# A mixture-of-experts decoder layer: in wide jobs VectorE turns the next job's rows in 32x32 blocks

## The chip, the cores and the metric

One NeuronCore of a Trainium2 chip runs the whole layer. The metric is the device time of one execution, in microseconds, as the median of three runs: 2102.54 us before the change (2101.25 to 2103.78).

## What is computed

The layer projects 1024 tokens of width 1024, runs sliding-window attention and a gated recurrence, projects back, and then routes each token to 4 of 32 experts. This case is about the experts only:

```python
logits = h @ router_w + router_b
top_v, top_e = lax.top_k(logits, 4)
gates = softmax(top_v)
# for every expert e, over the tokens routed to it:
hid = xblk @ w1[e] + b1[e]                      # 1024 -> 2048
glu = minimum(hid[:, 0::2], 7.0)
lin = clip(hid[:, 1::2], -7.0, 7.0)
act = glu * sigmoid(1.702 * glu) * (lin + 1.0)
y[tokens of e] += gate * (act @ w2[e] + b2[e])  # 1024 -> 1024
return rmsnorm(x + y, final_g)
```

All inputs are float32, and so is the output.

## The kernel before

**Jobs.** After routing (at some 650 us) the kernel works through jobs. A job is one expert and up to 160 of its tokens. There is room for `JOBS` = 57 jobs, and with these inputs 32 of them exist. Each of the five engines has its own loop over 57 iterations and does nothing in an iteration where `j < total` is false. A job of up to 128 tokens is *narrow* (`job(j, 1)`, 17 of the 32), one of 129 to 160 tokens is *wide* (`job(j, 2)`, 15 of the 32). From job 1 to job 15 and from job 18 to job 30 they take turns, so that a wide job always follows a narrow one, and a narrow one follows each wide one.

**Steps.** A job is 24 steps (`NS`), one for each 512 KB quarter of the expert's weights, in the order of `STREAM`: steps 0 to 15 are four units of `w1` (the up part), steps 16 to 23 two units of `w2` (the down part). Float32 products are made of float32r halves: ScalarE (ACT) copies a loaded quarter to `whi` (`jsplit`, L1406), VectorE (DVE) subtracts to get `wlo` (`jsplit`, L1970), and TensorE (PE) multiplies. There are 8 slots for `whi` and `wlo` and 12 for the raw quarters. At its step s ACT splits quarter s + 7 and DVE quarter s + 6, so DVE is some steps ahead of PE. SyncE (SP) loads a raw quarter as soon as `split_lo` says that a slot is free.

**Narrow and wide.** A narrow job has the tokens on the partitions of the product and turns its activations with PE (`a_turn`). A wide job has the hidden units on the partitions (`wide_step`, L1078 and L1080): eight groups of two matmuls a step, in six PSUM banks, `WIDE[g % 6]`. A bank that is used again has to be read first. This reading is DVE's `hidden_wide`: `sum_up` reduces the banks of a unit's first two groups to `gsum` and of its last two to `lsum`, each of which raises `sum_taken` by one (L2006). PE waits for it at the first step of a unit:

```python
if q == 0:
    if g >= 6:
        pe.wait_ge(sum_taken, j * 8 + (g - 6) // 2 + 1)
```

Group g = 6 is the third group of step 4 and waits for `gsum` of unit 0; groups 10 (step 8) and 14 (step 12) wait for `gsum` of units 1 and 2. DVE calls `hidden_wide` of unit c at its step 4c + 4, ahead of that step's split, and `activate_wide` behind the split.

**The next job's rows.** While job j runs, POOL (GpSimd) fetches the rows of job j + 1 from HBM by index: 128 rows of 4 KB to `xg` and the up to 32 further rows, in quarters of 1 KB, to `xq` (`gather`, L2219 and L2224). Both raise `gathered` by 16 when they have landed. They have to be turned, so that the model's width lies on the partitions. In both kinds of job PE does it, `x_turn(r)` with r = 0, 1 for `xg` (four 128x128 transposes each, at steps 18 and 19) and r = 2 for `xq` (two, at step 21), all on L1024. ACT and DVE take each result from PSUM as a high and a low half (`xT`, L1410 and L1993) at the same steps.

**POOL's order in a job** (from L2254): copy the kept indices and gates; wait until `xg` may be overwritten (`x_turned`); `gather(j + 1)`; load the slots of job j + 2; copy `icur`; wait for PE to have used the biases, load the next ones (`next_bias`); wait for ACT's last copy of the results (`y_set`); add the results to `acc_d` in HBM by index, with an indirect DMA (L2282). In a wide job the further 32 tokens' results are in two halves, rows 0 to 31 and 32 to 63 of `y[:, 1, :]`, which `y_fold` adds before the scatter. The wait for `y_set` is at the end of an iteration, and the gather is at the start of the next.

**The end.** After the last job SP loads the sums of the 8 token tiles, ACT squares them (L1507), DVE scales them (L2086), and SP stores them. ACT gets there after its empty iterations and loads a table first (L1502).

Of the kernel before, what the change touches and what calls it, by code (L numbers as in the profile page):

```python
# [25 lines left out]
P = 128  # L26
D = 1024
T = 1024
# [24 lines left out]
JT_W = JOBS + 2  # L53
PAD_ROWS = NE * SLOT_T // P
# [21 lines left out]
X_TURNS = 3  # L76
BIAS_AT = 3
# [18 lines left out]
def build(nc, x, norm1_g, w_in, b_in, attn_sinks, attn_out_g, hgrn_lb_logits, hgrn_out_g, w_out,  # L96
# [81 lines left out]
    xq = at("xq", B + 36 * KB, [P, D // 4])  # L178
    y = at("y", B + 40 * KB, [P, 2, D])
# [8 lines left out]
    yfold = at("yfold", B + 60 * KB, [HALF, 2, UNIT])  # L188
# [97 lines left out]
    with ctx:  # L286
# [60 lines left out]
        lin_set, yfolded, low_moved = sem("lin_set"), sem("yfolded"), sem("low_moved")  # L347
# [137 lines left out]
        def _(sp):  # L485
# [139 lines left out]
            with sp.Fori(0, JOBS, 1) as j:  # L625
                with sp.If(j < total):
                    e = sp.value_load(jobt[0:1, 0, bass.ds(j, 1)], min_val=0, max_val=NE - 1)
                    en = sp.value_load(jobt[0:1, 0, bass.ds(j + 1, 1)], min_val=0, max_val=NE - 1)
                    for s in range(RAWS, NS + RAWS):

                        wait(split_lo, j * NS + 4 * DENSE_UNITS + s - RAWS + 1)
                        c, q = STREAM[s % NS]
                        if s >= NS:
                            src = expert_part(w1v, q, en, slice(c * UNIT, (c + 1) * UNIT))
                        elif c < 4:
                            src = expert_part(w1v, q, e, slice(c * UNIT, (c + 1) * UNIT))
                        else:
                            src = expert_part(w2v, q, e, slice((c - 4) * UNIT, (c - 3) * UNIT))
                        sp.dma_start(raw_slot(s), src).then_inc(slot_in(s), 16)  # L639
# [11 lines left out]
        def _(pe):  # L651
# [383 lines left out]
            def biases(j):  # L1035
# [3 lines left out]
                pe.wait_ge(yfolded, j * 2 + 2)  # L1039
# [4 lines left out]
            def job(j, blocks):  # L1044
# [10 lines left out]
                def next_x(r):  # L1055
                    if r == 2:
                        pe.wait_ge(xT_lo, (j + 1) * X_TURNS + 1)
                    x_turn(r)
# [27 lines left out]
                for s in range(NS):  # L1086
# [36 lines left out]
                    if s in X_TURN_AT:  # L1123
# [1216 lines left out]
```

## Time and profile before

| | us |
|---|---|
| median of three runs | 2102.54 |
| the profiled execution, its own time | 2103.5 |
| its span, first to last instruction | 2101.9 |
| PE busy | 1970.8 (94%) |
| DVE busy | 1618.7 (77%) |
| ACT busy | 1312.8 (62%) |
| POOL busy | 631.3 (30%) |
| mean granted clock of PE | 0.973 |

The page gives for every engine the time in which it was busy, and its share of the span. PE's ends are modelled, so that a fully busy PE means that no matmul waited long, not that the array is at its peak. The granted clock is the share of the full 2.4 GHz; 0.5 is the lower of its two levels, 1.2 GHz. The windows view gives the busy time in chosen stretches, the lines view in groups of like instructions, and the timeline view gives instructions in order of time. An instruction's idle time in brackets is that of its engine just before it, with what ended it. Instructions of one engine can overlap by some 0.1 us, the end of one with the start of the next.

### The profile page before, as it was taken

Reading aid. Unit: us, or ns where it says so; the run is one execution under the profiler, and the core shown is the slowest. Engines: PE = TensorE matmul, PEld = TensorE weight load, DVE = VectorE, ACT = ScalarE, POOL = GpSimd, SP = SyncE. Lnnn points to the kernel's source line nnn. Section 1 sums busy time; section 2 is a strip of 40 time slices with the busy share of each in tenths; the row PEclk is TensorE's granted clock in tenths of the full one; section 3 lists DMA queues with packets and bytes.
Section 4 is the critical chain, followed back from the end, with each engine's and each line's share of the span. In section 5 each row is a group of like instructions: output and inputs, shape, how many; then the busy total and the mean of one; then the engine's idle time right before and its main releaser. Section 6 shows DMA issues by size and latency. Waiting matters only on the chain. (4 is left out here: it accounts for less than half of the span.)

```text
span 2101.9 us, 39974 instructions
## 1 busy us (share of the span) xinstructions
PE 1970.8 (94%) x11146; PEld 1686.6 (80%) x11147; DVE 1618.7 (77%) x2207; ACT 1312.8 (62%) x1912; POOL 631.3 (30%) x781
## 2 busy tenths in 40 slices
PE   7999988878977899999999999999999999999993
PEld 6887868867765879889798897979898888978882
DVE  5333157985657788989888898899888898988985
ACT  5221156553335676867768677787777676776765
POOL 3100011210225142523425244243424243332521
PEclk9999999999977999999999999999999999999997
DMA  5222120004256989989899898999899898998988
GB/s 191 67 81 61 50 101 2 21 11 137 81 191 215 317 285 313 328 269 372 275 322 317 275 373 268 336 308 374 281 344 302 294 345 272 351 294 305 335 271 304
DMA packets 265229, 506.50 MB, mean 241 GB/s; under 512 B 38550, under 2 KB 39574, under 8 KB 264916
## 3 DMA queue, kind: packets, MB, share of 16 engines
q1 hardware_dynamic: 243000, 457.91, 63.0%
q0 software_dynamic: 22176, 47.90, 9.0%
q8 instruction: 31, 0.51, 0.1%
q14 instruction: 22, 0.18, 0.0%
HBM read 466.50 MB, written 39.22 MB: 241 GB/s over the span
## 5 line engine op out<-in xcount | busy, mean ns | idle before, releaser
L1970 DVE TENSOR_TENSOR wlo<-raw,whi 128x1024 fp32r<-128x1024 f32 x774 | 956.8, 1260 | 64.1 <-ACT whi L1406 57.6
L1406 ACT ACTIVATE whi<-raw 128x1024 fp32r<-128x1024 f32 x775 | 844.6, 1116 | 143.8 <-PE ps L1080 103.5
L1078 PE MATMUL ps<-xT,whi 128*128 128x320 f32 x1920 | 504.2, 349 | 6.2 <-issue 5.7
L1080 PE MATMUL ps<-xT,wlo 128*128 128x160 f32 x1920 | 455.8, 237 | 0.0
L1078 PEld LDWEIGHTS ps<-xT,whi 128*128 128x128 f32 x1920 | 362.9, 189 | 10.0 <-issue 6.2
L1080 PEld LDWEIGHTS ps<-xT,wlo 128*128 128x128 f32 x1920 | 368.9, 192 | 0.4
L653 PE MATMUL ps<-whi,xT 128*128 128x512 f32 x544 | 218.4, 401 | 1.2 <-DVE xT L1993 1.2
L655 PE MATMUL ps<-whi,xT 128*128 128x512 f32 x544 | 213.5, 392 | 0.0
L653 PE MATMUL ps<-whi,aT 128*128 128x512 f32 x512 | 213.0, 416 | 0.2 <-DVE aTl L2031 0.2
L654 PE MATMUL ps<-wlo,xT 128*128 128x512 f32 x544 | 212.8, 391 | 0.0
L655 PE MATMUL ps<-whi,aTl 128*128 128x512 f32 x512 | 201.0, 393 | 0.0
L654 PE MATMUL ps<-wlo,aT 128*128 128x512 f32 x512 | 200.0, 391 | 0.0
L2282 POOL DMA_INDIRECT acc_d<-y,icur x64 | 113.5, 1774 | 207.9 <-ACT y L1441 173.4
L2189 POOL DMA_DIRECT2D brow<-brow_d x66 | 44.0, 764 | 297.8 <-PE ps L1080 281.8
L653 PEld LDWEIGHTS ps<-whi,xT 128*128 128x128 f32 x544 | 102.6, 189 | 26.6 <-issue 5.5
L655 PEld LDWEIGHTS ps<-whi,xT 128*128 128x128 f32 x544 | 102.5, 188 | 22.4
L654 PEld LDWEIGHTS ps<-wlo,xT 128*128 128x128 f32 x544 | 102.9, 189 | 20.3
L655 PEld LDWEIGHTS ps<-whi,aTl 128*128 128x128 f32 x512 | 96.1, 188 | 22.0
L1993 DVE TENSOR_TENSOR xT<-ps,xT 128x512 fp32r<-128x512 f32 (+1 forms) x99 | 59.3, 600 | 69.8 <-ACT xT L1410 69.8
L653 PEld LDWEIGHTS ps<-whi,aT 128*128 128x128 f32 x512 | 96.3, 188 | 20.2 <-DVE aTl L2031 0.5
L1540 DVE TENSOR_TENSOR wlo<-raw,whi 128x1024 fp32r<-128x1024 f32 (+1 forms) x24 | 27.1, 1134 | 107.8 <-ACT whi L1161 107.5
L654 PEld LDWEIGHTS ps<-wlo,aT 128*128 128x128 f32 x512 | 96.7, 189 | 15.9
(323 smaller groups left out, 3481.8 us busy)
## 6 DMA issues: line engine op xcount, KB each, us to landing
raw<-in_w SPq DMA_DIRECT2D x780, 512.0 KB
raw<-in_w_in SPq DMA_DIRECT2D x16, 512.0 KB
xs<-in_x SPq DMA_DIRECT2D x8, 512.0 KB, 10.4
raw<-in_w_out SPq DMA_DIRECT2D x8, 512.0 KB
mix<-in_x SPq DMA_DIRECT2D x8, 512.0 KB, 3.8
h_d<-h SPq DMA_DIRECT2D x8, 512.0 KB
acc_d<-mix SPq DMA_DIRECT2D x8, 512.0 KB
mix<-acc_d SPq DMA_DIRECT2D x8, 512.0 KB, 6.6
```

Source lines behind the costliest of these rows:

```text
L653: pe.matmul(o, sh, mh_, start=start, stop=False, skip_group_check=skip)
L654: pe.matmul(o, sh, ml_, start=False, stop=False, skip_group_check=skip)
L655: return pe.matmul(o, sl, mh_, start=False, stop=stop, skip_group_check=skip)
L1078: pe.matmul(o2, wh[:, a, cols], xT2[:, :, k, 0:JOB_T], start=q == 0 and a == 0, stop=False, skip_group_check=True)
L1080: m = pe.matmul(o, wl[:, a, cols], xT2[:, 0, k, 0:JOB_T], start=False, stop=q == QUARTERS - 1 and a == 1, skip_group_check=True)
L1406: act.activation(parted(slot(whis, s)), paired(raw_slot(s), s), ACT.Copy).then_inc(split_hi, 1)
L1540: dve.tensor_tensor(wl[:, q, :, 0:cols], raw[:, q, :, 0:cols], wh[:, q, :, 0:cols].bitcast(F32), ALU.subtract).then_inc(split_lo, 1)
L1970: dve.tensor_tensor(parted(slot(wlos, s)), paired(raw_slot(s), s), parted(slot(whis, s).bitcast(F32)), ALU.subtract).then_inc(split_lo, 1)
L1993: dve.tensor_tensor(turned_part(1, r), turned_bank(r), turned_part(0, r).bitcast(F32), ALU.subtract).then_inc(xT_lo, 1)
L2189: pool.dma_start(brow[low:P:32, 0:UNIT].bitcast(F32), bias_part(e, low)).then_inc(brow1_in, 16)
L2282: pool.indirect_dma_start(out=acc_d, out_offset=bass.IndirectOffsetOnAxis(ap=icur[0:n, b:b + 1], axis=0), in_=y[0:n, b, :], in_offset=None ...
```

## The change

1. In a wide job PE no longer turns `xg` of the next job. DVE does it with 16 `transpose` instructions, one after the split of each of its steps 3 to 18 (`x_move`), each of 32 partitions by 8 x 32 elements: it turns 32x32 blocks, and the 16 calls put the blocks in their places in a new tile `xturn` in SBUF. The first waits for `gathered`. At step 20 ACT copies the high half of all of it in one instruction, and DVE subtracts the low half in one (`xT_wide`). `xq` is still turned by PE, at step 19. Narrow jobs turn everything as before.
2. `y_fold` is gone. A wide job's two halves are scattered one after the other, the second when the first has landed, and then the 128 rows. A narrow job does two scatters of 4 rows in their place. `next_bias` comes first in both.
3. Each engine's loop is 3 groups of 19 iterations, a group is skipped when no job of it exists, and the second `If` became an `Else`.
4. Ahead of the loop ACT waits for `acc_out` after the first job's `xT` and not before.

```diff
+X_MOVE_FROM = 3
+X_TAKE_AT = 20
+X_LAST_AT = 19
+    xturn = at("xturn", B + 76.5 * KB, [P, KT, P])
-    yfold = at("yfold", B + 60 * KB, [HALF, 2, UNIT])
...
# PE
-                if s in X_TURN_AT:
+                    if blocks == 2 and s == X_LAST_AT:
+                        pe.wait_ge(gathered, j * 32 + 64)
+                        next_x(2)
+                    if blocks == 1 and s in X_TURN_AT:
...
-            with pe.Fori(0, JOBS, 1) as j:
-                with pe.If(j < total):
-                    left = pe.value_load(jobt[0:1, 2, bass.ds(j, 1)], min_val=0, max_val=T)
-                    with pe.If(left < P + 1):
-                        job(j, 1)
-                    with pe.If(left > P):
-                        job(j, 2)
+            with pe.Fori(0, GROUPS, 1) as g:
+                with pe.If(g * GROUP_JOBS < total):
+                    with pe.Fori(0, GROUP_JOBS, 1) as i:
+                        j = pe.snap(g * GROUP_JOBS + i)
+                        with pe.If(j < total):
+                            left = pe.value_load(jobt[0:1, 2, bass.ds(j, 1)], min_val=0, max_val=T)
+                            with pe.If(left < P + 1):
+                                job(j, 1)
+                            with pe.Else():
+                                job(j, 2)
...
# ACT
+            def xT_wide(j):
+                act.wait_ge(x_moved, j)
+                act.wait_ge(quarter_used, (j - 1) * NS + 4 * DENSE_UNITS + 16)
+                act.activation(xT2[:, 0, :, 0:P], xturn[:, :, :], ACT.Copy).then_inc(xT_hi, 2)
...
# DVE
+            def x_move(j, i):
+                if i == 0:
+                    dve.wait_ge(gathered, j * 32 + 32)
+                    dve.wait_ge(xT_hi, j * X_TURNS)
+                    dve.wait_ge(xT_lo, j * X_TURNS)
+                g, c = divmod(i, 4)
+                m = dve.transpose(xturn[32 * c:32 * c + 32, :, 32 * g:32 * g + 32],
+                                  xg[32 * g:32 * g + 32, :].rearrange("p (k c n) -> p k c n", c=4, n=32)[:, :, c, :])
+                if i == 15:
+                    m.then_inc(x_moved, 1)
+                    dve.wait_ge(x_moved, j)
+                    dve.sem_inc(x_turned, 2)
+
+            def xT_wide(j):
+                dve.wait_ge(xT_hi, j * X_TURNS + 2)
+                dve.wait_ge(x_moved, j)
+                dve.tensor_tensor(xT2[:, 1, :, 0:P], xturn[:, :, :], xT2[:, 0, :, 0:P].bitcast(F32),
+                                  ALU.subtract).then_inc(xT_lo, 2)
...
-                    for r in X_TURN_AT.get(s, ()):
-                        xT(j + 1, r)
+                    if blocks == 1:
+                        for r in X_TURN_AT.get(s, ()):
+                            xT(j + 1, r)
+                    elif 0 <= s - X_MOVE_FROM < 16:
+                        x_move(j + 1, s - X_MOVE_FROM)
+                    elif s == X_TAKE_AT:
+                        xT_wide(j + 1)
+                        xT(j + 1, 2)
...
# POOL
+                next_bias(j, e)
                 if blocks == 2:
-                    next_bias(j, e)
-                    y_fold(j, 4)
-                    y_fold(j, 5)
...
+                    wait(y_set[1], j * 2 + 4)
+                n = HALF if blocks == 2 else 4
+                scatter(n, y[0:n, 1, :], 1)
+                wait(scattered, j * 48 + 16)
+                scatter(n, y[HALF:HALF + n, 1, :], 1)
+                wait(y_set[0], j * 2 + 4)
+                scatter(P, y[:, 0, :], 0)
```

In the calls, `x_move` and `xT_wide` get j + 1, so `gathered, j * 32 + 32` there is the same value as PE's `gathered, j * 32 + 64`.

## Rows read from the trace of the kernel before

**Rows 1.** The page: the span, and busy time of PE and the others.
```profile
span 2101.9 us, 39974 instructions
PE 1970.8 (94%) x11146; PEld 1686.6 (80%) x11147; DVE 1618.7 (77%) x2207; ACT 1312.8 (62%) x1912; POOL 631.3 (30%) x781
```

**Rows 2.** Windows view (PE, PEld, DVE, ACT, POOL busy, clock, DMA): wide job, narrow job.
```profile
1889.30:1942.70 53.40, 53.38 (x349) 47.86 (x348) 43.63 (x57) 34.98 (x45) 13.40 (x19) 1.00 0.91 310
1942.70:1978.00 35.30, 35.30 (x166) 28.53 (x165) 34.61 (x39) 29.84 (x39) 19.63 (x22) 1.00 0.96 315
```

**Rows 3.** Timeline of PE (start, length) at that wide job's start and step 4.
```profile
1889.31 0.31 PE L1078 MATMUL ps<-xT,whi 128*128 128x320 f32 x1
...
1898.87 0.35 PE L1078 MATMUL ps<-xT,whi 128*128 128x320 f32 x1
```

**Rows 4.** Timeline of DVE in that job's steps 2 to 8, parts of it.
```profile
1893.92 2.38 DVE L1970 TENSOR_TENSOR wlo<-raw,whi 128x1024 fp32r<-128x1024 f32 x2
1896.99 0.82 DVE L2006 TENSOR_REDUCE gsum<-ps 128x320 f32<-128x640 f32 x1 [0.69 <-PE ps L1080]
1898.03 0.82 DVE L2006 TENSOR_REDUCE lsum<-ps 128x320 f32<-128x640 f32 x1 [0.21 <-PE ps L1080]
...
1899.51 0.33 DVE L2025 TENSOR_SCALAR lsum<-lsum 128x320 f32<-128x320 f32 x1
1899.75 1.27 DVE L1970 TENSOR_TENSOR wlo<-raw,whi 128x1024 fp32r<-128x1024 f32 x1
...
1902.95 2.35 DVE L1970 TENSOR_TENSOR wlo<-raw,whi 128x1024 fp32r<-128x1024 f32 x2
1905.31 0.82 DVE L2006 TENSOR_REDUCE gsum<-ps 128x320 f32<-128x640 f32 x1
```

**Rows 5.** Lines view of 700 to 2101 us: PE's transposes of xg.
```profile
L1024 PE MATMUL ps<-ident,xg 128*128 128x128 f32 x248 | 37.1, 272 | 0.0
```

**Rows 6.** Timeline of POOL around that wide job's start, parts of it.
```profile
1891.28 1.85 POOL L2282 DMA_INDIRECT acc_d<-y,icur  x1 [10.35 <-ACT y L1441]
1892.96 1.09 POOL L2256 CAST ikept<-tkept 128x2 int32<-128x2 f32 x1
...
1897.22 1.04 POOL L2219 DMA_INDIRECT xg<-h_d,inext  x1 [0.86 <-POOL inext L2217]
...
1899.42 1.01 POOL L2224 DMA_INDIRECT xq<-h_d,inext  x1 [0.81 <-POOL inext L2222]
```

**Rows 7.** DMA view, software queue: 1896.4 to 1900, 1901.4 to 1903, 1903 to 1904.6.
```profile
q0 software_dynamic: 144, 0.52, 72.9%
...
q0 software_dynamic: 103, 0.42, 65.2%
...
q0 software_dynamic: 89, 0.23, 37.8%
```

**Rows 8.** Timeline: the first job's gather on POOL and its first turn on PE.
```profile
644.16 1.03 POOL L2224 DMA_INDIRECT xq<-h_d,inext  x1 [0.82 <-POOL inext L2222]
...
647.40 1.97 PE L1024 MATMUL ps<-ident,xg 128*128 128x128 f32 x8 [0.85 <-DMA xq<-h_d,inext]
```

**Rows 9.** Lines view of 700 to 2101 us: a one-source DVE operation of 256 elements.
```profile
L2000 DVE TENSOR_SCALAR lin<-ps 128x256 f32<-128x256 f32 x64 | 26.6, 416 | 0.0
```

**Rows 10.** Windows view (columns of rows 2): a pause of PE and what followed.
```profile
692.00:698.00 6.00, 0.42 (x2) 0.00 (x0) 3.53 (x3) 2.72 (x4) 2.97 (x4) 0.83 1.05 384
698.00:702.70 4.70, 4.55 (x19) 4.55 (x20) 0.00 (x0) 0.39 (x1) 2.48 (x4) 0.50 1.07 293
702.70:707.00 4.30, 4.30 (x34) 4.30 (x34) 2.39 (x2) 2.11 (x3) 3.10 (x6) 1.00 1.03 400
```

**Rows 11.** Timeline: the gather of xg in the following narrow job, and its first turn.
```profile
1953.91 1.14 POOL L2219 DMA_INDIRECT xg<-h_d,inext  x1 [0.87 <-POOL inext L2217]
...
1969.71 0.60 PE L1024 MATMUL ps<-ident,xg 128*128 128x128 f32 x4
```

**Rows 12.** Timeline of ACT after its last job.
```profile
2083.95 1.28 ACT L1502 ACT_TABLE_LOAD   x1 [15.99 <-issue]
```

**Rows 13.** Windows view (columns of rows 2) of the end.
```profile
2076.00:2087.60 11.60, 0.00 (x0) 0.00 (x0) 0.65 (x2) 3.61 (x6) 0.00 (x0) 0.50 0.93 362
2087.60:2089.00 1.40, 0.00 (x0) 0.00 (x0) 1.36 (x3) 1.37 (x4) 0.00 (x0) 0.50 0.00 0
```

**Rows 14.** Timeline of DVE ahead of the first job.
```profile
650.59 0.91 DVE L2067 MEMSET y<- 128x1024 f32 x1 [0.16 <-issue]
651.46 1.29 DVE L1993 TENSOR_TENSOR xT<-ps,xT 128x512 fp32r<-128x512 f32 x2
```

More of the change, by code:

```diff
@@ L624, in _ @@
             third_unit(3)
[L625 to L639, printed above, removed]
+            with sp.Fori(0, GROUPS, 1) as g:
+                with sp.If(g * GROUP_JOBS < total):
+                    with sp.Fori(0, GROUP_JOBS, 1) as i:
+                        j = sp.snap(g * GROUP_JOBS + i)
+                        with sp.If(j < total):
+                            e = sp.value_load(jobt[0:1, 0, bass.ds(j, 1)], min_val=0, max_val=NE - 1)
+                            en = sp.value_load(jobt[0:1, 0, bass.ds(j + 1, 1)], min_val=0, max_val=NE - 1)
+                            for s in range(RAWS, NS + RAWS):
+                                wait(split_lo, j * NS + 4 * DENSE_UNITS + s - RAWS + 1)
+                                c, q = STREAM[s % NS]
+                                if s >= NS:
+                                    src = expert_part(w1v, q, en, slice(c * UNIT, (c + 1) * UNIT))
+                                elif c < 4:
+                                    src = expert_part(w1v, q, e, slice(c * UNIT, (c + 1) * UNIT))
+                                else:
+                                    src = expert_part(w2v, q, e, slice((c - 4) * UNIT, (c - 3) * UNIT))
+                                sp.dma_start(raw_slot(s), src).then_inc(slot_in(s), 16)
             sp.wait_ge(jobs_over, 1)
@@ L1038, in biases @@
                 pe.wait_ge(y_set[0], j * 2 + 2)
[L1039 removed]
+                pe.wait_ge(y_set[1], j * 2 + 2)
                 for u in range(4):
@@ L1055, in next_x @@
                 def next_x(r):
-                    if r == 2:
+                    if r == 2 and blocks == 1:
                         pe.wait_ge(xT_lo, (j + 1) * X_TURNS + 1)
@@ L1479, in _ @@
             gates_hi(NT - 1)
-            for i in range(2):
-                act.wait_ge(acc_out[i], 64)
             act.wait_ge(jobs_set, 1)
@@ L1486, in _ @@
                 act.sem_inc(y_set[b], 2)
-            act.sem_inc(yfolded, 2)
             for r in range(X_TURNS):
                 xT(0, r)
+            for i in range(2):
+                act.wait_ge(acc_out[i], 64)
             for s in range(4, AHEAD_HI):
                 jsplit(0, s)
-            with act.Fori(0, JOBS, 1) as j:
-                with act.If(j < total):
-                    left = act.value_load(jobt[0:1, 2, bass.ds(j, 1)], min_val=0, max_val=T)
-                    with act.If(left < P + 1):
-                        job(j, 1)
-                    with act.If(left > P):
-                        job(j, 2)
+            with act.Fori(0, GROUPS, 1) as g:
+                with act.If(g * GROUP_JOBS < total):
+                    with act.Fori(0, GROUP_JOBS, 1) as i:
+                        j = act.snap(g * GROUP_JOBS + i)
+                        with act.If(j < total):
+                            left = act.value_load(jobt[0:1, 2, bass.ds(j, 1)], min_val=0, max_val=T)
+                            with act.If(left < P + 1):
+                                job(j, 1)
+                            with act.Else():
+                                job(j, 2)
             act.activation(spare[:, 0:1], epsc[:, 0:1], ACT.Sqrt)
@@ L2051, in job @@
                         aT_wide(j, WIDE_TURN_AT[s])
-                    for r in X_TURN_AT.get(s, ()):
-                        xT(j + 1, r)
+                    if blocks == 1:
+                        for r in X_TURN_AT.get(s, ()):
+                            xT(j + 1, r)
+                    elif 0 <= s - X_MOVE_FROM < 16:
+                        x_move(j + 1, s - X_MOVE_FROM)
+                    elif s == X_TAKE_AT:
+                        xT_wide(j + 1)
+                        xT(j + 1, 2)
                 if blocks == 2:
```

66 lines of the change are left out of this document (31 added, 35 removed).

## The prediction, made before the changed kernel was run

> **What bounds the kernel now.** I read the page first: a span of 2101.9 us with TensorE (PE) busy 94% and VectorE (DVE) 77% [rows 1]. Then the windows view over one wide job and the narrow job after it, in the expert stage: PE is busy 53.38 of 53.40 us and 35.30 of 35.30 us at full clock, while DVE works 43.63 and 34.61 us [rows 2]. Wide and narrow jobs nearly alternate: 17 narrow, 15 wide, 32 in all. So every microsecond by which PE waits inside a job is a microsecond of the span, and DVE has little air: 10 us in a wide job, under 1 us in a narrow one. Next I read one wide job instruction by instruction, on PE, DVE and POOL, because the change gives DVE a new thing to wait for at the job's third step.
>
> PE starts this job at 1889.31, and its 128 pairs of matmuls of the up part follow each other 0.26 us apart: eight pairs a step, 2.08 us, four steps a unit, 8.32 us. The pair that starts at 1898.87, 9.6 us into the job, is the first of step 4 that writes a bank of unit 0 again [rows 3]; it waits for `sum_taken`, DVE's `gsum` reduction of unit 0. Before, that reduction ran at 1896.99 to 1897.81 [rows 4], a microsecond early.
>
> **Part 1, the turns leave PE.** Eight transposes of `xg` go in each wide job. Two turns of four each take 37.1 / 62 = 0.60 us a turn, and one transpose alone is 0.27 [rows 5], so one costs (0.60 - 0.27) / 3, some 0.1 us of PE's time in the stream: 0.8 us a wide job, 15 x 0.8 = **12 us gained**, on the bounding engine.
>
> **Part 2, a new wait on DVE.** `x_move(j + 1, 0)` stands behind the split of DVE's step 3 and waits for `gathered`, both gathers of the next job's rows. Before, only PE's step 18 needed them, 35 us later. When do they land? POOL issues them only after it has issued the scatter of the job before, which waits for ScalarE's last copy of that job. In this job the scatter is issued at 1891.28, the gather of `xg` at 1897.22 and that of `xq` from 1899.42 to 1900.43 [rows 6]. The software queue moves the scatter's 0.52 MB by 1900, then 0.42 MB from 1901.4 to 1903 and 0.23 MB by 1904.6 [rows 7]: together 0.65 MB, which is 128 rows of 4 KB and 128 of 1 KB. They have landed at 1904.4, **15.0 us** after PE's start of the job; the 14 wide jobs after the first repeat these times within 0.1 us (33 gathers of each kind in all). DVE's split of step 3, the second of the pair ahead of `gsum`, ends at 1896.3 [rows 4], 7.0 us into the job. The change leaves this chain on POOL as it is behind a narrow job, and every wide job but none else follows a narrow one. So DVE stands still for 8 us, and behind it in its queue stands `gsum` of unit 0.
> Then: one move (0.33, below) and `gsum` (0.82) end at 15.0 + 0.33 + 0.82 + 0.1 for the semaphore, at 16.3 us. PE wanted it at 9.6 and waits **6.7 us**. Bounds of the landing: without other traffic the gathers landed 2.2 us after the issue's end (645.19 to 647.40) instead of 4.0 [rows 8]; SyncE's loads also dry up while DVE stands still, so 13.3 us is the early end, a pause of 5.0; 1.5 us later than now is the other.
>
> **Part 3, the moves' own cost.** No transpose on DVE is in the trace. The nearest row is a one-source operation of the same 256 elements a partition, 416 ns [rows 9]; two splits of 1.22 us take 2.35 together [rows 4], so instructions overlap by 0.09, and the move takes 0.33 us of DVE's time. That is the value I take; 0.24 is the low end (L2025, SBUF to SBUF, 320 elements: the next instruction starts 0.24 after it [rows 4]), 0.60 the high end (most of the 0.82 us that the reduction needs for 640 elements).
> The Trainium skill has a price for it: "VectorE: DVE Perf Modes", section on the three transpose paths, gives 311 ns for a 128x128 bf16 tile in 32x32 blocks, and "Vector Engine (DVE) Microarchitecture Reference", section 3.8, one element per cycle and lane. As an estimate from these pages 256 elements would be 0.44 us, 0.35 in the stream, and the sum below would grow by 2 us. No run here shows it yet.
> One unit of the up part lasts 8.32 us on PE, and DVE works all of it but 0.21 us (from `gsum` at 1896.99 to `gsum` at 1905.31 [rows 4]): 8.11. With four moves it is 8.11 + 4 x 0.33 = 9.43. PE cannot run ahead of this, because the third group of each of the steps 8 and 12 again waits for the `gsum` of the unit before. So PE passes that point of step 12 at 16.3 + 2 x 9.43 = 35.2 us instead of 9.6 + 2 x 8.32 = 26.2: **9.0 us late**, of which 6.7 is the pause. After step 12 nothing waits for `gsum`; in the down part PE needs 2.5 us a step (53.4 less 16 x 2.08, by 8) and DVE 1.2 to 1.6, so the lag ends there, with `xT_wide` (one split-sized subtraction, 1.22, in place of two of 0.69) beneath the same cover. If that cover were gone it would cost 1 us a job.
>
> **Part 4, the clock.** PE's one pause of this size among the jobs, 692.4 to 698.1, was followed by half clock: in 698 to 702.7 PE ran 19 matmuls at 0.50, in the next 4.3 us 34 at 1.00 [rows 10]. So 4.7 us held 2.4 us of work and 2.3 us were lost. I expect this after each pause. But it is no new term: 6.7 + 2.3 = 9.0, and DVE's pace has PE at 9.0 late anyway. The larger of the two counts. It holds up the low end: with moves at 0.24 DVE's lateness would be 8.2, and the clock's 8.9 would stand.
>
> **Part 5, POOL.** The fold (two copies, two adds) leaves a wide job's end; in its place is a scatter of 32 rows, the wait until it has landed, a second one, and then the scatter of 128. A scatter's issue is 1.85 and its landing came 8.6 us after the issue's start for 128 rows [rows 6, 7]; for 32 rows I take 6 to 8.6. Before, the gather of `xg` was issued at 1953.91, in the narrow job behind; I expect it 3 to 5 us later, landed by 1967.5 at the latest. PE turns those rows at 1969.71 [rows 11], so this is hidden, with 2 us to spare, and costs 1 for 1 beyond. In a narrow job two small scatters lie ahead of the wait for `y_set[0]`, for which POOL sat idle 10.35 us [rows 6]; they and the landing between need about 8. Nothing.
>
> **Part 6, loops and ends.** ScalarE runs 25 empty iterations after the last job before its table load at 2083.95, an idle time of 15.99 us, 0.58 us each [rows 12]. With groups of 19 it runs 6 and skips a group: about 11 us less. The rows to be normalized come first from memory: these loads begin at 2076 and fill the DMA engines to 2087.6 [rows 13]. Their first tile is there at some 2079, and the stores then share the queue, so what can be saved is between the 1.4 us in which the DMA stood idle (2087.6 to 2089) and 6 us. **3 us gained.** The moved wait for `acc_out` on ScalarE: DVE takes the first turned rows at 651.46, directly behind its own memset [rows 14], so an earlier copy gains nothing (bound: 0 to 1 us). Fewer comparisons per job (`Else`) lie under queued work.
>
> **The sum.** 14 wide jobs lose 9.0 - 0.8 = 8.2 us: +115. The first wide job starts only after a pause of its own, and its gathers land when DVE gets there; it loses some 1.2 to DVE's pace and gains 0.8: +0.4. The tail: -3. The profiled execution took 2103.5 us (a span of 2101.9 and 1.6 around it), 1 us above the median of 2102.5. The sum is 2103.5 + 115.4 - 3 = 2215.9 for such an execution, and **2215 us** for the median, 5.3% slower.
>
> **Rivals.**
> A, the other side: the gathers are there when DVE asks, by 8 us into the job, so nothing pauses. Then DVE's pace alone decides: 7.0 + 0.33 + 0.82 + 18.9 = 27.0 against 26.2, 0.8 late, eaten by the 0.8 gained: 2102.5 - 3 = 2100; with moves at 0.24 there is no lateness and the 12 us come in full, 2088. It needs POOL 7 us earlier. Against it: the chain ACT copy, scatter, casts, gather is dependent throughout [rows 6]; for it: POOL's casts of two words last 1.1 us beside a busy DVE. Chance 0.07 for faster, 0.04 for 2100, no change.
> The Trainium skill speaks for rival A: "VectorE: DVE Perf Modes", rules for kernel authors, names VectorE the fastest for 32x32 blocks, and its table has 311 ns against TensorE's 390. That rule prices the operation alone, and says nothing of what stands behind it in the queue.
> B, the moves cost 0.60: 16.55 + 2 x 10.51 = 37.6, 11.4 late, 10.6 a job: +148, less the tail, 2248. Chance 0.15.
> C, the landing is early (13.3) since loads dry up: the pause is 5.0, DVE's lateness 7.3, the clock's 7.3; 6.5 a job: 2191. Chance 0.17.
> D, POOL's new order holds up a narrow job's scatter of 128 rows by the landing of the small ones, up to 3 us, and with it the gather that the wide job waits for: 14 x 3 more, 2257. Chance 0.05.
> The forecast itself: 0.52.
>
> **Range and chances.** Eight in ten lie from C's lower side to B's upper: 2182 to 2252. A measurement here tells about 0.2%, 4 us, from no change. Faster 0.07, same 0.04, slower 0.89.
>
> **What will show it.** Right: a pause of 6 to 7 us on PE in each wide job but the first, released by DVE's `gsum`; DVE idle some 8 us ahead of the first transpose of the job, released by the DMA of `xq`; the granted clock at one half after it; wide jobs of 61 to 62 us and narrow ones of 35.3; transposes of 0.42 us x240. Wrong: a gather issued before DVE's step 3, a transpose over 0.7, or PE pauses at the narrow jobs' step 18.

## The result and the profile after

The changed kernel takes **2255.81 us** (2253.11 to 2258.07, 4 runs) against 2102.41 (2101.25 to 2103.78, 4 runs) before: ratio 1.073, 95% interval 1.0717 to 1.0743. That is 153 us slower; 113 were predicted, and the range ended 4 us short. The profiled execution took 2253.1 us, 149.6 more than that of before.

The page of after, span and busy times, to be set beside [rows 1]:

```profile
span 2251.5 us, 39516 instructions
...
PE 1989.7 (88%) x11026; PEld 1702.1 (76%) x11027; DVE 1694.8 (75%) x2432; ACT 1314.3 (58%) x1897; POOL 594.2 (26%) x753
```

PE's share fell from 94 to 88%. The windows view over one wide job and the narrow job behind it (columns as in [rows 2]):

```profile
1187.40:1251.00 63.60, 54.70 (x340) 48.93 (x339) 50.26 (x71) 34.16 (x43) 12.15 (x18) 0.92 0.76 250
1251.00:1286.50 35.50, 35.50 (x167) 28.79 (x166) 32.91 (x39) 30.70 (x40) 18.20 (x20) 1.00 0.99 333
```

The narrow job is as before. The wide one is 10 us longer, and PE works 54.7 of its 63.6 us, at a mean clock of 0.92. From PE's start of a wide job to its start of the next narrow one, 53.05 us have become 63.65 on average in twelve jobs and 65.5 in two; the first wide job went from 55.00 to 56.75. The 16 narrow jobs behind the first take 35.59 on average for 35.70, 1.8 us less together. The first wide job starts 1.2 us sooner, which is within what this start varies from trace to trace (696.9 to 700.8 us), and the end is 1.4 us shorter. This adds up to 12 x 10.6 + 2 x 12.45 + 1.75 - 1.8 - 1.2 - 1.4 = 149.5 us, which is the whole difference between the two executions.

What PE waits for, and what DVE waits for (waits view: us in total, times, longest), and the lines view of the new transposes:

```profile
PE ps L1087 <- DVE gsum L2051: 130.5, 30, 9.8
```
```profile
DVE xturn L2028 <- DMA xq<-h_d,inext: 137.7, 15, 11.4
...
L2028 DVE STREAM_TRANSPOSE xturn<-xg 32x256 f32<-32x256 f32 x240 | 104.6, 436 | 144.7 <-DMA xq<-h_d,inext 137.7
```

Before, no wait of PE for `gsum` and none of DVE for a gather stood in this view. One wide job shows the chain; PE starts it at 1187.37. POOL, DVE and PE in the timeline (start, duration, what, in brackets the idle time before and its releaser). The second row's bracket names ScalarE's copy, but the program has POOL wait there for the landing of the first small scatter:

```profile
1181.72 1.78 POOL L2302 DMA_INDIRECT acc_d<-y,icur  x1 [0.97 <-POOL bcur L2289]
1188.92 2.13 POOL L2302 DMA_INDIRECT acc_d<-y,icur  x1 [5.41 <-ACT y L1461]
1191.35 1.88 POOL L2302 DMA_INDIRECT acc_d<-y,icur  x1 [0.30 <-issue]
...
1196.08 1.03 POOL L2274 DMA_INDIRECT xg<-h_d,inext  x1 [0.88 <-POOL inext L2272]
...
1198.28 1.00 POOL L2279 DMA_INDIRECT xq<-h_d,inext  x1 [0.83 <-POOL inext L2277]
```
```profile
1193.15 1.23 DVE L1995 TENSOR_TENSOR wlo<-raw,whi 128x1024 fp32r<-128x1024 f32 x1 [0.25 <-ACT whi L1421]
1203.91 0.43 DVE L2028 STREAM_TRANSPOSE xturn<-xg 32x256 f32<-32x256 f32 x1 [9.54 <-DMA xq<-h_d,inext]
1204.28 0.77 DVE L2051 TENSOR_REDUCE gsum<-ps 128x320 f32<-128x640 f32 x1
...
1208.24 0.43 DVE L2028 STREAM_TRANSPOSE xturn<-xg 32x256 f32<-32x256 f32 x1
1208.69 1.23 DVE L1995 TENSOR_TENSOR wlo<-raw,whi 128x1024 fp32r<-128x1024 f32 x1
...
1214.20 0.78 DVE L2051 TENSOR_REDUCE gsum<-ps 128x320 f32<-128x640 f32 x1
...
1224.12 0.77 DVE L2051 TENSOR_REDUCE gsum<-ps 128x320 f32<-128x640 f32 x1
```
```profile
1205.11 0.64 PE L1087 MATMUL ps<-xT,whi 128*128 128x320 f32 x1 [8.00 <-DVE gsum L2051]
```

DVE has split step 3 by 1194.4, 7.0 us into the job. Then it stands before its first transpose, for 9.54 us, until the gathers have landed, and `gsum` of unit 0 stands behind it. PE, which wanted that `gsum` at 9.6 us into the job, resumes at 17.75. DVE's `gsum` to `gsum` is 9.92 us, twice; the third frees PE's step 12 at 37.6, where it was 26.2 before. That is 11.4 us late, less 0.8 us for the turns that PE no longer does: the 10.6.

When the rows landed, in the DMA view (packets, MB, share) of the software queue over 1200.5 to 1203.15 and over 1203.15 to 1203.9:

```profile
q0 software_dynamic: 180, 0.61, 56.5%
...
q0 software_dynamic: 1, 0.00, 0.1%
```

The last rows are in at 1203.15, and the transpose starts at 1203.91. Between the last data packet and the start of the waiting instruction lie 0.8 us.

### The profile page after: what moved, and what is told of

Read it like the earlier page. It is cut to its first block, busy times and chain, and to the rows that moved or that the text cites. A ratio compares the mean times of both kernels' runs of the same rounds, so it can differ in the third digit from the quotient of the medians.

```text
span 2251.5 us, 39516 instructions
## 1 busy us (share of the span) xinstructions
PE 1989.7 (88%) x11026; PEld 1702.1 (76%) x11027; DVE 1694.8 (75%) x2432; ACT 1314.3 (58%) x1897; POOL 594.2 (26%) x753
## 4 chain that ended last, share of the span: by engine, by line
PE 21%; issue 14%; DMA 12%; POOL 10%; DVE 9%; POOLq 2%; ACT 1%; DVEq 0%; SPq 0%; ACTq 0%
DMA acc_d<-y,icur 8%; PE ps L1087 4%; DMA xq<-h_d,inext 4%; PE ps L662 3%; PE ps L664 3%; PE ps L663 3%; DVE wlo L1995 3%; POOL acc_d L2302 3%; PE ps L1127 2%; PE ps L1128 2%; DVE xturn L2028 2%; PE ps L1089 2%; POOL xg L2274 1%; DVE gsum L2051 1%; POOL tnext L2267 1%
## 5 line engine op out<-in xcount | busy, mean ns | idle before, releaser
L1995 DVE TENSOR_TENSOR wlo<-raw,whi 128x1024 fp32r<-128x1024 f32 x774 | 930.1, 1221 | 82.2 <-ACT whi L1421 65.6
L1087 PE MATMUL ps<-xT,whi 128*128 128x320 f32 x1920 | 538.6, 364 | 136.6 <-DVE gsum L2051 130.5
L1087 PEld LDWEIGHTS ps<-xT,whi 128*128 128x128 f32 x1920 | 382.0, 199 | 146.1 <-DVE gsum L2051 136.3
L1089 PE MATMUL ps<-xT,wlo 128*128 128x160 f32 x1920 | 468.1, 244 | 0.0
L1089 PEld LDWEIGHTS ps<-xT,wlo 128*128 128x128 f32 x1920 | 388.0, 202 | 0.5
L2302 POOL DMA_INDIRECT acc_d<-y,icur x96 | 181.1, 1887 | 412.2 <-ACT y L1464 223.3
L2028 DVE STREAM_TRANSPOSE xturn<-xg 32x256 f32<-32x256 f32 x240 | 104.6, 436 | 144.7 <-DMA xq<-h_d,inext 137.7
L1440 ACT ACTIVATE sigw<-gsum,bcur 128x160 f32<-128x160 f32 x120 | 44.9, 421 | 258.9 <-DVE gsum L2051 258.9
L2244 POOL DMA_DIRECT2D brow<-brow_d x66 | 37.7, 573 | 474.8 <-PE ps L1089 437.8
L663 PEld LDWEIGHTS ps<-wlo,aT 128*128 128x128 f32 x512 | 96.7, 189 | 17.3
```

What stands on the lines that cost most here:

```text
L663: pe.matmul(o, sh, ml_, start=False, stop=False, skip_group_check=skip)
L1087: pe.matmul(o2, wh[:, a, cols], xT2[:, :, k, 0:JOB_T], start=q == 0 and a == 0, stop=False, skip_group_check=True)
L1089: m = pe.matmul(o, wl[:, a, cols], xT2[:, 0, k, 0:JOB_T], start=False, stop=q == QUARTERS - 1 and a == 1, skip_group_check=True)
L1440: m = act.activation(sigw[:, i, :], gsum[:, i, :], ACT.Gelu_apprx_sigmoid, bias=bcur[:, 0, 2 * c + i:2 * c + i + 1])
L1995: dve.tensor_tensor(parted(slot(wlos, s)), paired(raw_slot(s), s), parted(slot(whis, s).bitcast(F32)), ALU.subtract).then_inc(split_lo, 1)
L2028: m = dve.transpose(xturn[32 * c:32 * c + 32, :, 32 * g:32 * g + 32], xg[32 * g:32 * g + 32, :].rearrange("p (k c n) -> p k c n", c=4, n=3 ...
```

## The experiments

Theory W: the place of the wait does it. DVE waits for a landing some 9 us away, with a reduction behind it that PE needs; the transposes' time is the smaller part, and the rest of the change costs nothing. The rivals: the transposes are dear wherever they stand (M), POOL's new order does it (P), the half clock after the pause adds to it (K).

**The moves late.** The 16 transposes at steps 12 to 19, two a step, when the rows are there; all else as changed.

```diff
-X_MOVE_FROM = 3
+X_MOVE_FROM = 12
-                    elif 0 <= s - X_MOVE_FROM < 16:
-                        x_move(j + 1, s - X_MOVE_FROM)
+                    elif 0 <= s - X_MOVE_FROM < 8:
+                        for i in range(2):
+                            x_move(j + 1, 2 * (s - X_MOVE_FROM) + i)
```

> The changed kernel with its 16 moves at DVE's steps 12 to 19, two a step, in place of one a step from 3 to 18. The gathers of the next job land some 16 us into a wide job and DVE's step 12 begins after 24 us, so nothing is waited for; unit 3 and the down part give DVE room, as no group of PE waits for gsum of unit 3. If the wait for the gather at step 3 is the cause (theory W): no pause on PE, wide jobs of 52.3 us, narrow ones of 35.6, time 2087 us (2082 to 2092), faster than before by 0.7%. If the cause is the load of the moves on DVE wherever they stand (rival M): wide jobs stay over 55 us, time over 2130.

Measured: 2109.5 us (2107.56 to 2111.36, 6 runs), ratio 1.0036 [1.0024, 1.0049]. With the same 240 transposes 146 of the 153 us are gone: W, against M. Wide jobs last 52.42 us, as expected; none has a pause. But the time is 22 us over what was expected. Some 14 of them are the narrow jobs', which take 36.5 on average (36.7 behind most wide jobs) where 35.6 was expected; the end of the span saves nothing either (35.1 us behind PE's last matmul, 33.5 in the changed kernel). The waits view, which had no such row before, and POOL at the end of a wide job:

```profile
PE ps L1033 <- DMA xq<-h_d,inext: 11.2, 14, 1.3
```
```profile
1112.28 1.45 POOL L2303 DMA_INDIRECT acc_d<-y,icur  x1 [15.13 <-ACT y L1464]
1120.53 2.06 POOL L2303 DMA_INDIRECT acc_d<-y,icur  x1 [6.80 <-DMA acc_d<-y,icur]
1122.89 1.72 POOL L2303 DMA_INDIRECT acc_d<-y,icur  x1 [0.30 <-issue]
...
1128.01 1.44 POOL L2275 DMA_INDIRECT xg<-h_d,inext  x1 [0.87 <-POOL inext L2273]
```

The second scatter of 32 rows waits 8.25 us for the landing of the first, the gather goes out 15.7 us after the first scatter, and PE, no longer delayed, comes to the narrow job's step 18 a microsecond before the rows. This is the cost that Part 5 of the prediction called hidden "with 2 us to spare". In the changed kernel it is hidden, and by just these 2 us: the rows land 25 us into the narrow job, and PE turns them at 27.3. The length of the wide job is not the reason, for the same holds in the run with all but the moves (below), whose wide jobs last 53.0. With late moves POOL's first scatter comes 1.1 us later, behind a later last copy of ScalarE (3.5 us into the narrow job for 2.3), and holds up the second by 7.8 to 8.6 us instead of 5.7 to 6.6, so the gather goes out at 19.2 for 15.9. Why this landing takes longer there wasn't tested.

**The wait alone.** The kernel before, with DVE waiting at step 3 and nothing to do there.

```diff
+                    if blocks == 2 and s == 3:
+                        dve.wait_ge(gathered, j * 32 + 64)
                     for r in X_TURN_AT.get(s, ()):
                         xT(j + 1, r)
```

> The kernel before with one added line: in a wide job DVE waits for both gathers behind the split of its step 3. No moves, POOL as before. Theory W: gathers land at 15.0 us, DVE is released 0.8 later as in the changed kernel, gsum ends at 16.6, PE pauses 7.0 in 14 wide jobs. DVE's pace is 8.1 a unit and can't hold PE up further, so here the half clock after the pause must show as a term of its own, 2.2: wide jobs of 62.3, 14 x 9.2 more, time 2231 us. If the clock costs nothing: 2200.

Measured: 2235.35 us (2234.73 to 2236.19, 4 runs), ratio 1.0633 [1.0615, 1.065]. One wait costs 133 us. The rows land at 15.0 us into the job, `gsum` starts at 15.7, and PE resumes at 16.6. Windows view of the pause and of what follows (PE, PEld, DVE, ACT, POOL busy, granted clock, DMA share, GB/s):

```profile
1191.10:1198.20 7.10, 0.28 (x3) 0.10 (x1) 0.98 (x2) 0.04 (x1) 4.04 (x8) 0.69 1.04 380
1198.20:1202.90 4.70, 4.70 (x20) 4.70 (x21) 4.54 (x9) 3.33 (x5) 0.00 (x0) 0.50 0.58 164
1202.90:1207.20 4.30, 4.30 (x31) 4.30 (x31) 2.35 (x2) 2.04 (x2) 0.00 (x0) 0.87 0.78 242
```

Behind the pause PE runs at half clock for a while. Its third group of step 8 comes 27.4 us into the job on average (26.5 to 28.1) instead of 16.6 + 8.3 = 24.9: 7.0 for the pause and 2.5 for the clock, times 14, are the 133 us. Without transposes DVE has time to spare, so here the clock's loss does come on top.

**No wait, but the moves.** The transposes at their changed places, from a tile that is always there (so the experts after the first compute with wrong rows).

```diff
-                    dve.wait_ge(gathered, j * 32 + 32)
-                                  xg[32 * g:32 * g + 32, :].rearrange(
+                                  grow[32 * g:32 * g + 32, :].rearrange(
```

> The changed kernel, but the moves turn the blocks of a tile that nobody writes in this stage (grow) and don't wait for the gather; so the further experts compute with wrong rows, and the time is that of the moves at steps 3 to 18 without the wait. Work per unit on DVE is 9.92 us in the changed kernel's trace against PE's 8.32. Theory W with DVE's pace: gsum of unit 2 ends 8.5 + 2 x 9.92 = 28.3 us into the job where PE wants it at 26.2, 2.1 late less the 0.8 gained: wide jobs of 54.3, time 2119 us (2108 to 2125). Rival M: over 2180.

Measured: 2125.57 us (2124.04 to 2127.17, 4 runs), ratio 1.0107 [1.009, 1.0124]. `gsum` of unit 0 is in time, PE's third groups of steps 8 and 12 come at 18.8 and 28.75 instead of 17.9 and 26.2, and a wide job lasts 54.75. The transposes' time at these steps, with the rest of the change, is worth 23 us. The 6 us above expectation are 0.45 a job: I had counted two units of 9.92 us from `gsum` to `gsum`, but the first takes 10.3 (1160.59 to 1170.89 in one job), for DVE's reductions of unit 0 still wait for PE's matmuls there (0.35 us before `gsum`, 0.21 before `lsum`).

**The pause filled.** 40 matmuls into an unused bank ahead of PE's wait, so that the clock stays up.

```diff
+                            if g == 6:
+                                for i_ in range(40):
+                                    pe.matmul(ps[:, 7, 0:2 * JOB_T].rearrange("p (h n) -> p h n", h=2), wh[:, 0, 0:P],
+                                              xT2[:, :, 0, 0:JOB_T], start=True, stop=True, skip_group_check=True)
```

> The changed kernel with 40 matmuls of 128x320 into an unused PSUM bank ahead of the group that waits, so that PE works through its pause (40 x 0.19 = 7.5 of 8.0 us) and keeps its clock. Their result is not used. In the first wide job, which has no pause, they cost 6 to 7 us. If DVE's pace sets the lateness by step 12 and the half clock is hidden under it, as the prediction had it: time 2256 + 7 = 2263 us, wide jobs of 63.6. If the clock's loss comes on top: 2.2 less in each of 14 jobs, 2232.

Measured: 2258.25 us (2255.74 to 2260.54, 4 runs), ratio 1.0739 [1.0721, 1.0757]. First the windows of the changed kernel, then those of this one:

```profile
1197.10:1205.10 8.00, 0.00 (x1) 0.00 (x0) 1.19 (x3) 0.00 (x0) 4.30 (x10) 0.65 1.02 339
1205.10:1209.70 4.60, 4.59 (x19) 4.60 (x20) 4.49 (x7) 3.35 (x5) 0.00 (x0) 0.50 0.20 48
1209.70:1214.00 4.30, 4.30 (x35) 4.30 (x35) 4.18 (x8) 2.32 (x2) 0.00 (x0) 1.00 0.76 243
```
```profile
1201.40:1209.40 8.00, 5.90 (x41) 5.64 (x39) 1.13 (x3) 0.00 (x0) 4.33 (x10) 1.00 1.04 345
1209.40:1214.00 4.60, 4.54 (x23) 4.54 (x24) 4.49 (x8) 3.32 (x5) 0.00 (x0) 0.65 0.31 72
...
1191.70:1255.30 63.60, 60.03 (x379) 54.23 (x378) 50.29 (x71) 33.81 (x43) 12.11 (x18) 0.97 0.77 253
```

The clock of the wide job is 0.97 instead of 0.92, and the job is no shorter: 63.6 us. PE is at step 8's third group 0.5 us earlier (27.7 for 28.2) and at step 12's at 37.6 in both. Against K: DVE's pace hides the clock's loss in the changed kernel. The kernel's 2.4 us more are less than what the first wide job alone lost to the filling, 4 us.

**All but the moves.** The changed kernel with PE turning all rows in wide jobs again; the edit on DVE, with its like on PE and ACT:

```diff
-                    if blocks == 1:
-                        for r in X_TURN_AT.get(s, ()):
-                            xT(j + 1, r)
-                    elif 0 <= s - X_MOVE_FROM < 16:
-                        x_move(j + 1, s - X_MOVE_FROM)
-                    elif s == X_TAKE_AT:
-                        xT_wide(j + 1)
-                        xT(j + 1, 2)
+                    for r in X_TURN_AT.get(s, ()):
+                        xT(j + 1, r)
```

> The changed kernel with PE turning everything again as before: what is left of the change is POOL's scatters and the loops. The end should save 1.4 us. In the run with late moves PE waited 1.05 us in 13 narrow jobs at step 18 for gathers that POOL had issued late, behind the landing of the 32-row scatter. If that is POOL's doing alone (theory W with POOL's term), it shows here too: narrow jobs of 36.7, time 2115 us. If it came with the moves: narrow jobs of 35.7 and 2101 us.

Measured: 2100.35 us (2098.45 to 2102.03, 10 runs), ratio 0.999 [0.998, 1.0]. Against P: the scatters and the loops alone cost nothing. Narrow jobs last 35.6, as under the second outcome named, so the microsecond that they lost in the run with late moves came with the moves. Its windows, a wide and a narrow job:

```profile
1187.40:1240.40 53.00, 52.92 (x267) 43.09 (x266) 45.05 (x50) 42.25 (x54) 23.20 (x24) 1.00 0.94 310
1240.40:1276.00 35.60, 35.60 (x248) 33.28 (x247) 31.28 (x46) 23.21 (x30) 9.04 (x16) 1.00 0.96 322
```

Yet its gather goes out 8.7 us into the wide job, as in the changed kernel, and not at 7.9 as before. Where nobody waits for it, the 0.8 us are free.

**The loops alone.** The kernel before with groups of 19 iterations and `Else`.

```diff
-            with pe.Fori(0, JOBS, 1) as j:
-                with pe.If(j < total):
+            with pe.Fori(0, GROUPS, 1) as g:
+                with pe.If(g * GROUP_JOBS < total):
+                    with pe.Fori(0, GROUP_JOBS, 1) as i:
+                        j = pe.snap(g * GROUP_JOBS + i)
...
-                    with pe.If(left > P):
+                            with pe.Else():
```

> The kernel before with the loops in three groups and Else, nothing else. In the changed kernel ACT's table load came 6.3 us after PE's last matmul instead of 17.0, and the span's end 33.5 after it instead of 34.9. Theory: 1.4 us gained, 2101 us; the prediction had 3, 2099.5.

Measured: 2100.88 us (2098.01 to 2102.61, 11 runs), ratio 0.9995 [0.9986, 1.0004]. 1.3 us less, which this interval doesn't tell from nothing; 3 were predicted for it. In its trace the end of the span comes 32.2 us behind PE's last matmul, for 34.9 before.

**POOL's share within the change.** The changed kernel with the old fold on POOL and one scatter for the further rows; in the code of POOL's job:

```diff
-                wait(scattered, j * 48 + 16)
-                scatter(n, y[HALF:HALF + n, 1, :], 1)
+                    y_fold(j, 4)
+                    y_fold(j, 5)
```

> The changed kernel with POOL's work as before (fold, no wait for landing), moves still at steps 3 to 18. POOL's term by itself: the gather of xg is issued at 7.9 us instead of 8.7 in 12 jobs and 10.3 in two, so 0.8 less in 12 jobs and 2.4 in two: wide jobs of 62.8, time 2256 - 14 = 2241 us. If POOL's order has no part in it: 2256.

Measured: 2246.34 us (2244.96 to 2247.05, 4 runs), ratio 1.0685 [1.0667, 1.0703]. The gather goes out at 7.9 again, lands at 15.0, and the first transpose starts at 15.8. So POOL's new order is worth 9.5 us of the 153: P as a part. 14 us were expected. The two jobs whose gather had gone out at 10.35 gained the 2.4 expected, but the twelve others only 0.5 and not 0.8, for here the half clock shows: step 8 is as late as in the changed kernel (28.0), and step 12 is reached at 37.25 for 37.6.

**One step later.** `X_MOVE_FROM = 4`, so that `gsum` of unit 0 is ahead of the wait.

```diff
-X_MOVE_FROM = 3
+X_MOVE_FROM = 4
```

> The changed kernel with the moves at DVE's steps 4 to 19. The wait for the gather now stands behind gsum and lsum of unit 0. Theory W: DVE is released at 16.6 us as before, does four moves, three splits and one take in 6 us, gsum of unit 1 ends at 23.3 where PE wants it at 17.9; at a pace of 9.9 gsum of unit 2 ends at 33.2 against 26.2, 7.0 late less the 0.8: wide jobs of 59.3, 4.3 less than in the changed kernel, time 2194 us. If the place of the wait made no difference: 2255.

Measured: 2208.18 us, a single run, so without an interval. PE is in time at step 4 (9.6) and waits at step 8 instead (24.1 for 17.9); in most jobs step 12 comes at 34.2, 3.4 us sooner than in the changed kernel. The wait takes its toll one unit later, on the reduction that then stands behind it. It is 14 us more than expected: in most jobs DVE starts its moves at 17.3 and not 16.6, and a unit takes it 10.05 us from `gsum` to `gsum`, not 9.92. Why the rows land 0.7 later than in the changed kernel wasn't tested.

**Late moves, old fold.** Late moves as above, POOL's fold as before, to keep the gather early.

```diff
-X_MOVE_FROM = 3
+X_MOVE_FROM = 12
...
-                wait(scattered, j * 48 + 16)
-                scatter(n, y[HALF:HALF + n, 1, :], 1)
+                    y_fold(j, 4)
+                    y_fold(j, 5)
```

> Moves late (steps 12 to 19, two a step), loops in groups, and POOL's work as in the kernel before (fold, one scatter behind the other without a wait for landing). Theory: wide jobs of 52.4, narrow ones of 35.7, the end 1.4 us shorter: 2102.5 - 15 x 0.65 - 1.4 = 2091 us, faster than before by 0.5%. If the late moves cost something of their own in narrow jobs: 2105.

Measured: 2124.54 us (2122.74 to 2125.45, 4 runs), ratio 1.0105 [1.0088, 1.0122], 33 us more than expected. Wide jobs last 52.42, narrow ones 37.8. Waits view:

```profile
PE ps L663 <- DVE aTl L2079: 24.2, 16, 1.5
```

PE now waits for DVE's part of the activations within the narrow job. Take as DVE's lead the time from the end of a split to the start of the step in which PE uses it. In the kernel before it is 13.3 us at a narrow job's start and 4.9 at its smallest. With the moves at steps 12 to 19 the narrow job starts with 7.3. Without the fold its smallest is 4.9 again; with the fold, which POOL runs beside DVE in the narrow job's first steps, it falls to 3.1. The timeline and lines views show where it goes: three splits beside the fold, three in the run with late moves alone, and POOL's add here and in the kernel before:

```profile
1206.21 5.43 DVE L1998 TENSOR_TENSOR wlo<-raw,whi 128x1024 fp32r<-128x1024 f32 x3
```
```profile
1201.69 3.50 DVE L1995 TENSOR_TENSOR wlo<-raw,whi 128x1024 fp32r<-128x1024 f32 x3 [0.52 <-ACT whi L1421]
```
```profile
L2310 POOL TENSOR_TENSOR y<-y,yfold 32x512 f32<-32x512 f32 x30 | 64.4, 2148 | 2.5
```
```profile
L2251 POOL TENSOR_TENSOR y<-y,yfold 32x512 f32<-32x512 f32 x30 | 38.6, 1288 | 2.5
```

The two engines lengthen each other's instructions: three splits take 5.43 us instead of 3.50, and an add of the fold 2.15 us instead of 1.29 in the kernel before, where DVE has pauses beside it. That the lost lead is what makes the activations late, and not the slower instructions in some other way, is argued. Late moves are not free: they spend a lead that the next job wants.

**Late moves, the second half deferred.** POOL scatters the second half only after the next gather, and that of the last job behind its 128 rows.

```diff
                 with pool.If(j > 0):
                     wait(scattered, j * 48)
+                    scatter(HALF, y[HALF:2 * HALF, 1, :], 1)
...
                 scatter(n, y[0:n, 1, :], 1)
-                wait(scattered, j * 48 + 16)
-                scatter(n, y[HALF:HALF + n, 1, :], 1)
```

> Late moves (steps 12 to 19) with the changed kernel's scatters, except that POOL issues the second half of a job's further rows only in its next iteration, after the gather; nothing waits for a landing ahead of the gather (one scatter of four rows of zeros is added ahead of the loop). Theory: the run with late moves lost 1.05 us in narrow jobs to a gather that landed late, and the run with late moves and the fold lost 2.1 to DVE, which has no room in a narrow job and is slowed by the fold on POOL. Without both, wide jobs 52.4 and narrow ones 35.6: 2091 us. If DVE's work alone is what late moves run into: narrow jobs of 36.5 or more, over 2103.

Measured: **2096.14 us** (2094.71 to 2100.02, 8 runs) against 2102.18 (18 runs), ratio 0.9975 [0.9965, 0.9986]. It beats both kernels. POOL at the end of a wide job, and the windows over a wide and a narrow one:

```profile
1109.55 1.42 POOL L2303 DMA_INDIRECT acc_d<-y,icur  x1 [15.09 <-ACT y L1464]
1111.27 2.38 POOL L2303 DMA_INDIRECT acc_d<-y,icur  x1 [0.31 <-issue]
...
1117.32 1.10 POOL L2275 DMA_INDIRECT xg<-h_d,inext  x1 [0.88 <-POOL inext L2273]
```
```profile
1053.70:1106.10 52.40, 52.34 (x340) 46.54 (x338) 48.44 (x70) 32.84 (x42) 13.54 (x18) 1.00 0.90 308
1106.10:1141.70 35.60, 35.60 (x166) 28.85 (x167) 34.81 (x41) 31.22 (x41) 18.11 (x20) 1.00 0.97 329
```

The gather follows the first scatter by 7.8 us instead of 15.7, PE never pauses in these jobs, and the wide job is 0.65 us shorter than before. That is what the change can give: 14 x 0.65 = 9 us of Part 1's 12. PE's last matmul ends 8.3 us earlier than before (2058.6 for 2067.0); the end of the span comes 37.2 us after it and not 34.9, which takes 2.2 back and leaves 6. The trace shows why: the last job's half is scattered last of all, when the 128 rows have landed, and the loads of the sums wait for it.

```profile
2060.39 1.58 POOL L2303 DMA_INDIRECT acc_d<-y,icur  x1 [3.98 <-ACT y L1461]
2067.21 1.32 POOL L2303 DMA_INDIRECT acc_d<-y,icur  x1 [5.23 <-DMA acc_d<-y,icur]
```
```profile
2070.87 4.16 SPq L652 DMA_DIRECT2D mix<-acc_d  x8
```

These loads start 12.2 us behind PE's last matmul, 3.7 later than before (8.5), and from there to the end it takes 24.9 us, 1.5 less than before.

**Late moves, packed tighter.** The same with three moves a step at steps 12 to 15 and two at 16 and 17, to win back lead.

```diff
+                    elif 12 <= s < 18:
+                        for i in range(3 * (s - 12), 3 * (s - 11)) if s < 16 else range(2 * s - 20, 2 * s - 18):
+                            x_move(j + 1, i)
```

> As the deferred scatter with late moves, but the moves stand three a step at 12 to 15 and two a step at 16 and 17, so that DVE has six steps of the down part to win back its lead before the narrow job. If the lead at the start of the narrow job decides (7.3 us with moves to step 19, 13.3 before the change): narrow jobs no longer than there, and the time 2091 us or up to 5 less than the other run's where that one is over 2095. If the moves in unit 3 delay lsum of unit 3, PE waits at step 18: wide jobs of 54, 2112 us.

Measured: 2119.18 us (2117.44 to 2119.71, 5 runs), ratio 1.008 [1.0067, 1.0094]: the second of the outcomes named. Wide jobs last 54.0, by this row of the waits view:

```profile
PE ps L662 <- DVE lsum L2051: 23.3, 15, 1.6
```

Twelve moves before the last reduction of the up part make it 1.6 us late for the first matmuls of the down part. 0.45 us more in each of four steps decides between the best kernel and one slower by 0.8%.

## Where the prediction was right, and where it failed

**The mechanism held.** DVE waits for the gathers with `gsum` behind it, PE waits for `gsum`, then DVE's pace sets PE's step 12, and the down part is untouched. The wait alone gave 133 us, and the change without the wait 23, of which -2 are the rest (all but the moves) and so 25 the transposes: together 156, for the measured 153. That they add up so well is in part chance, for the first holds 2.5 us a job for the clock, which the changed kernel hides, and POOL's later gather, worth 9.5, shows only where somebody waits for it.

**Where the 37 us went** that the profiled execution took beyond the 2215.9 of the sum. The forecast failed in its sizes, and the time lay outside the range. Four terms were wrong, all to the same side:

- Part 2, "0.1 for the semaphore": from the last packet of the rows to the start of the waiting instruction it is 0.8 us, in the wait alone 0.7. I had the time of the last packet [rows 7] and took it for the release. +0.7 a job.
- Part 5, "Nothing" for a narrow job's small scatters: the second goes out 7.2 us after the first (1181.72 to 1188.92), 1.5 us into the wide job, and the scatter of 128 rows and then the gather come behind it, 0.8 us later than before (8.7 for 7.9 us into the job). I had put "about 8" for them into 10.35 us of idle time [rows 6] and did not ask when the first of them could start: it goes out 5.65 us ahead of the wide job. This is rival D's mechanism, at 0.8 instead of "up to 3". In two of the jobs this first scatter goes out 1.9 us later still, behind a pause of POOL among the loads of the slots, and they lost 1.9 more; the landing took no longer there (7.1 us).
- Part 3, the move at 0.33: it lasts 436 ns, and the next split starts 0.45 after it (1208.24 to 1208.69), so nothing overlaps. I had carried over the 0.09 us by which two splits overlap. A unit of DVE is 9.92 us, which is 8.11 + 4 x 0.45, and not 9.43: +1.0 over the two units.
- Part 6, 3 us at the end: ScalarE's table load does come early, 6.3 us after PE's last matmul instead of 17.0, but the end moved by 1.4. From the first load of the sums to the end it takes 24.2 us for 26.4 before, so 2.2 were gained (the other traces with the new loops have 23.9 to 25.7 there), but these loads start 9.3 us after PE's last matmul and not 8.5. With the old scatters they start at 8.4 under the new loops too (the loops alone, the changed kernel with the old fold): the other 0.8 is the new scatters' and stood nowhere in the sum. (The 15.99 us over 25 iterations are also 0.64 each, not 0.58; nothing hangs on it.)

A job is thus 0.7 + 0.75 + 1.0 = 2.4 us later than the 9.0 of the sum, 14 x 2.4 = 34; with 3.7 for the two jobs, 1.4 more in the first wide job and 1.6 at the end, less 1.8 in the narrow jobs and 1.2 ahead of the first wide one, it is 38.

Rival C's early landing did not come. SyncE's loads ran on through PE's pause (DMA share 1.02 in the windows above) and dried up only behind it (0.20), and the last rows were in at 15.8 us, not 13.3.

The trace of after shows 436 ns for a transpose of 256 elements a partition. "Vector Engine (DVE) Microarchitecture Reference" of the Trainium skill, section 3.8, has one element per cycle and lane, and "VectorE: DVE Perf Modes" of the Trainium skill, section on the three transpose paths, 311 ns for a 128x128 bf16 tile; the 0.44 us estimated from the two is what the trace shows, and only the overlap that I took off was wrong. The rule in "VectorE: DVE Perf Modes" of the Trainium skill, rules for kernel authors, that VectorE is fastest for 32x32 blocks, is neither shown nor contradicted by the runs: moving them to late steps took 146 us off, while their time where they stood was worth some 25.

**Part 4, the clock**, was right as put: half clock after each pause, and no new term. The filled pause shows it. In most jobs it did hold up step 8 (28.2 for the 27.7 of the filled pause), but in most of them step 12 came no later.

**Part 1** was right in size, 0.65 of 0.8 us a job in the best kernel. **Part 5's** cover of 2 us for the gather in the narrow job was right in the changed kernel; with late moves it was gone, and that cost a microsecond a job.

**The range** was too narrow at its upper end by the way it was made: each rival took one cost at its high end and left the others at the value taken. Rival B alone ended at 2248 and D at 2257; the true time lay at half of B's step, a quarter of D's and a release that no rival held. Three small costs on one chain, each with a bound above only, ought to have been added.

## What to carry to other kernels

Before an engine is given a wait for data, read what stands behind it in its queue and when the data land: here one wait at the wrong step cost 133 us, and the transposes taken off the bounding engine gave 9 in the jobs and 6 in the whole, at best. Move such work to where its input is long there, but then count how much lead the engine has left at the next stage, since late work is paid from it. For a chain of dependent steps, add their high ends when the range is made.

## What the hardware showed unexpectedly

- From the last packet of an indirect gather to the start of the DVE instruction that waited for it: 0.8 us in the changed kernel, 0.7 with the wait alone.
- How long a scatter takes to land doesn't follow its number of rows closely. In the changed kernel 4 rows held up the next scatter by 7.0 to 7.7 us and 32 rows by 5.7 to 6.6; with late moves 32 rows held it up by 7.8 to 8.6; 128 rows took some 8.6 to their last packet [rows 6, 7].
- A DVE transpose of 32 x 256 float32 takes 436 ns and is not overlapped by the split behind it (0.45 us in the stream), while two splits overlap by 0.09.
- POOL's copies and adds at the start of a narrow job cost DVE 1.8 us of its lead (4.9 to 3.1) in the kernel with late moves: three splits of DVE take 5.43 us beside them and 3.50 without them, and POOL's adds 2.15 us instead of 1.29.
